# Expert turns on split weights: gate and up in slabs of 512 columns, two weight tiles to a slab

## What is computed

```
def swiglu(h, w_gate, w_up, w_down):
    return (jax.nn.silu(h @ w_gate) * (h @ w_up)) @ w_down

logits = (t @ router).astype(F32)
top_v, top_i = lax.top_k(logits, TOP_K)        # TOP_K = 2 of N_EXPERTS = 8
gates = jax.nn.softmax(top_v, axis=-1)
def run_block(args):
    tok, e = args
    return swiglu(t[tok], w_gate[e], w_up[e], w_down[e])
...
y = jnp.zeros_like(t).at[slot_tok].add(out)
```

## Time and profile before

| | us |
|---|---|
| median of 3 runs | 2563.54 |
| lowest, highest | 2558.66, 2566.74 |
| the profiled execution, its own time | 2564.95 |
| span of the profiled execution | 2563.1 |
| PE busy | 2330.8 (91%) |
| DVE busy | 1191.1 (46%) |
| ACT busy | 926.1 (36%) |

### The profile page before, as it was taken

How to read it: one execution, slowest core, us unless ns; L and a number is a source line. 1 busy time by engine, 2 the same in 40 slices (tenths; PEclk the granted TensorE clock), 3 DMA queues, 4 the chain that set the end, 5 groups by cost and what they waited for, 6 DMA issues and landing times.

```text
span 2563.1 us, 41521 instructions
## 1 busy us (share of the span) xinstructions
PE 2330.8 (91%) x17097; PEld 2067.9 (81%) x17097; DVE 1191.1 (46%) x1606; ACT 926.1 (36%) x1176; POOL 118.5 (5%) x182
## 2 busy tenths in 40 slices
PE   7988999999999777778969999999999999999995
PEld 6864888888778666645959898988899999999995
DVE  3267433232353666534368887888888100001001
ACT  4346322221322333134236666676667000000001
POOL 6010000000000000000000000000000100000000
PEclk9999899999999888889879999999999999999998
DMA  6310232242221000020179999999999877877663
GB/s 183 121 66 17 67 99 88 93 136 91 74 90 38 2 2 2 2 66 1 75 239 339 336 339 336 343 343 343 346 342 320 284 256 240 266 258 249 230 224 115
DMA packets 334011, 452.37 MB, mean 176 GB/s; under 512 B 8392, under 2 KB 291887, under 8 KB 333711
## 3 DMA queue, kind: packets, MB, share of 16 engines
q1 hardware_dynamic: 328896, 435.73, 50.8%
q0 software_dynamic: 4752, 14.00, 2.3%
q10 hardware_dynamic: 190, 0.05, 0.0%
HBM read 437.22 MB, written 12.52 MB: 175 GB/s over the span
## 4 chain that ended last, share of the span: by engine, by line
PE 84%; DVE 7%; ACT 4%; issue 2%; DMA 1%; ACTq 0%; DVEq 0%; POOLq 0%; SPq 0%; POOL 0%
PE bank L668 81%; PE bank L671 4%; DVE arena L1899 2%; DVE slot L1899 1%; DVE w_low L1899 1%; ACT w_high L1816 1%; DVE h_mix L1899 0%; DVE small L1952 0%; ACT arena L1585 0%; ACT w_high L1427 0%; DMA arena<-h_rows_d,idx_ahead 0%; DMA xs<-sum_rows_d 0%; DMA sum_rows_d<-arena,idx_now 0%; ACT arena L1459 0%; DVE arena L2576 0%
## 5 line engine op out<-in xcount | busy, mean ns | idle before, releaser
L1899 DVE TENSOR_TENSOR w_low<-slot,w_high 128x2048 fp32r<-128x2048 f32 x172 | 393.6, 2292 | 314.7 <-ACT w_high L1427 266.4
L668 PE MATMUL bank<-arena 128*128 128x144 f32 (+7 forms) x2608 | 349.6, 300 | 6.4 <-ACT arena L1502 2.6
L668 PE MATMUL bank<-w_high,xg_high 128*128 128x256 f32 x1120 | 325.9, 291 | 11.3 <-issue 4.8
L668 PE MATMUL bank<-arena,slot 128*128 128x144 f32 (+4 forms) x2368 | 313.2, 312 | 20.6 <-ACT slot L1733 14.8
L668 PEld LDWEIGHTS bank<-arena 128*128 128x128 f32 (+4 forms) x2608 | 308.5, 185 | 22.4 <-issue 11.0
L668 PEld LDWEIGHTS bank<-arena,slot 128*128 128x128 f32 (+2 forms) x2368 | 290.4, 189 | 39.8 <-issue 19.7
L668 PE MATMUL bank<-w_low,xg_high 128*128 128x256 f32 x1120 | 318.6, 284 | 0.0
L668 PE MATMUL bank<-w_high,xg_low 128*128 128x256 f32 x1120 | 317.9, 284 | 0.0
L1899 DVE TENSOR_TENSOR arena<-arena,bank 128x256 f32<-128x256 f32 (+3 forms) x134 | 63.8, 476 | 528.7 <-PE bank L668 528.7
L1899 DVE TENSOR_TENSOR w_low<-arena,w_high 128x2048 fp32r<-128x2048 f32 x105 | 240.5, 2291 | 55.7 <-ACT w_high L1816 55.7
L1816 ACT ACTIVATE w_high<-slot 128x2048 fp32r<-128x2048 f32 x108 | 207.0, 1918 | 78.3 <-PE bank L668 49.5
(11 more groups left out here) (365 smaller groups left out, 3398.7 us busy)
## 6 DMA issues: line engine op xcount, KB each, us to landing
slot<-in_moe_w_gate_dram SPq DMA_DIRECT2D x64, 1024.0 KB, 6.1
arena<-in_moe_w_down_dram SPq DMA_DIRECT2D x64, 1024.0 KB, 5.8
slot<-in_moe_w_up_dram SPq DMA_DIRECT2D x56, 1024.0 KB, 5.8
arena<-in_moe_w_up_dram SPq DMA_DIRECT2D x56, 1024.0 KB, 6.5
arena<-in_moe_w_gate_dram SPq DMA_DIRECT2D x48, 1024.0 KB, 5.8
slot<-in_moe_w_down_dram SPq DMA_DIRECT2D x48, 1024.0 KB, 6.3
slot<-in_e_w_in_dram SPq DMA_DIRECT2D x12, 1024.0 KB, 5.6
slot<-in_ff_w_gate_dram SPq DMA_DIRECT2D x11, 1024.0 KB, 5.4
```

Of the source, the lines that this page charges most:

```text
L668: return pe.matmul(o, lhsT, rhs, start=start, stop=True, skip_group_check=True)
L1899: return dve.tensor_tensor(o, a, b, op)
```

## The change

In split turns alone, gate and up are worked in slabs of 512 columns. A slab is two tiles, each of four row blocks (512 rows) by 512 columns, still 1 MB; PE works a tile as 4 x 3 matmuls 512 columns wide, and both tiles add into one full bank. The order (`wide_order`) becomes g0 g1 u0 u1, then six times two g, two u and two d, where the d are those of the slab before; the last two are d12 d13. SiLU and `hid_tok` are formed once a slab, 512 columns wide, into single buffers. `turn_hidden(p-2)` stands behind g(p), and the last two stand behind d10 and d11. At the turn's end ACT takes `hid_high` ahead of `xg_parts`, not behind. The positions (7, 10, 16, 19, 22) of the row work are kept as numbers. The 16 matmuls on the identity ahead of the first turn become 28. The float32 turns are as they were but for their first six loads, which wait for a count that holds after either order (`former_tile_used`).

```
+def wide_order():
+    slab = lambda j: [("g", 2 * j), ("g", 2 * j + 1), ("u", 2 * j), ("u", 2 * j + 1)]
+    w = slab(0)
+    for j in range(1, GROUPS_E // 2):
+        w += slab(j) + [("d", 2 * j - 2), ("d", 2 * j - 1)]
+    return w + [("d", GROUPS_E - 2), ("d", GROUPS_E - 1)]
+def former_tile_used(n):
+    return ([("up_full", FF_TILES)] * 2 + [("down_used", 9)] * 3 + [("down_used", 10)])[n]
...
-                            name, count = expert_tile_used(n - RAW)
+                            name, count = former_tile_used(n) if n < RAW else expert_tile_used(n - RAW)
...
+                        if kind in ("g", "u") and split:
+                            rows, cols = 512 * (j % 2), 512 * (j // 2)
...
-                            for k in range(KT):
-                                m = split_product(b[:, 0:256], (xg_high[:, k, :], xg_low[:, k, :]), (wh[:, k, :], wl[:, k, :]), k == 0)
+                            for k in range(4):
+                                row = 4 * (p % 2) + k
+                                m = split_product(b[:, :], (xg_high[:, row, :], xg_low[:, row, :]), (wh[:, k, :], wl[:, k, :]), row == 0)
...
-                                if j >= 1:
-                                    turn_hidden(j - 1)
+                                if p >= 2:
+                                    turn_hidden(p - 2)
...
-                                if j == GROUPS_E - 1:
-                                    turn_hidden(j)
-                                down(n, j)
+                                down(n, p)
+                                if p in (GROUPS_E - 4, GROUPS_E - 3):
+                                    turn_hidden(p + 2)
...
-                for i in range(16):
+                for i in range(28):
                     mm(acc[0][:, 0:P], ident[:, :], ident[:, :], True)
...
-                            if kind == "g":
-                                act.wait_ge(sem("gate_full"), turn * GROUPS_E + (FF_TILES + j + 1))
-                                act.wait_ge(sem("hid_ready"), turn * GROUPS_E + (FF_TILES + j - 1))
-                                act.activation(sil_e[:, j % 2, 0:256], turn_banks[2 * j % 4][:, 0:256], ACT.Silu)\
+                            if kind == "g" and p % 2 == 1:
+                                act.wait_ge(sem("gate_full"), turn * GROUPS_E + (FF_TILES + p + 1))
+                                act.wait_ge(sem("hid_ready"), turn * GROUPS_E + (FF_TILES + p - 1))
+                                act.activation(sil_wide[:, :], turn_banks[(p - 1) % 4][:, :], ACT.Silu).then_inc(sem("sil_ready"), 2)
...
-                                tt(hid_tok[:, j % 2, :], sil_e[:, j % 2, 0:256], turn_banks[(1 + 2 * j) % 4][:, 0:256], ALU.mult)\
+                                tt(hid_tok[:, :], sil_wide[:, :], turn_banks[p % 4][:, :], ALU.mult).then_inc(sem("hid_ready"), 2)
```

More of the change, by code:

```diff
@@ L481, in expert @@
                     ring = expert_ring(raw_slots, landed, turn)
-                    for n, (kind, j) in enumerate(expert_order()):
+                    for n, (kind, j) in enumerate(wide_order() if split else expert_order()):
                         if split:
@@ L1812, in high @@
                         if ring.turn is not None:
-                            name, count = expert_tile_used(n - SPLIT)
+                            name, count = wide_tile_used(n - SPLIT)
                             act.wait_ge(sem(name), turn * GROUPS_E + count)
@@ L1826, in expert_split @@
                         ring.n = SPLIT
-                        for n, (kind, j) in enumerate(expert_order()):
-                            if kind == "g":
-                                act.wait_ge(sem("gate_full"), turn * GROUPS_E + (FF_TILES + j + 1))
-                                act.wait_ge(sem("hid_ready"), turn * GROUPS_E + (FF_TILES + j - 1))
-                                act.activation(sil_e[:, j % 2, 0:256], turn_banks[2 * j % 4][:, 0:256], ACT.Silu)\
[L1832 to L1837, removed]
+                        for n, (kind, p) in enumerate(wide_order()):
+                            if kind == "g" and p % 2 == 1:
+                                act.wait_ge(sem("gate_full"), turn * GROUPS_E + (FF_TILES + p + 1))
+                                act.wait_ge(sem("hid_ready"), turn * GROUPS_E + (FF_TILES + p - 1))
+                                act.activation(sil_wide[:, :], turn_banks[(p - 1) % 4][:, :], ACT.Silu).then_inc(sem("sil_ready"), 2)
+                            turned = p - 2 if kind == "g" and p >= 2 else p + 2 if kind == "d" and GROUPS_E - 4 <= p < GROUPS_E - 2 else -1
                             if turned >= 0:
@@ L1843, in expert_split @@
                                                ACT.Copy).then_inc(sem("hid_high_ready"), 1)
+                            if n == TILES_E - 3:
+                                act.wait_ge(sem("up_full"), turn * GROUPS_E + (FF_TILES + GROUPS_E))
+                                xg_parts(turn, 1)
                             if n < TILES_E - 2:
@@ L2490, in expert_split @@
                         rows_after = {17: 0, 20: 1, 23: 2}
-                        for n, (kind, j) in enumerate(expert_order()):
-                            turned = j - 1 if kind == "g" else j if j == GROUPS_E - 1 and kind == "d" else -1
+                        for n, (kind, p) in enumerate(wide_order()):
+                            turned = p - 2 if kind == "g" and p >= 2 else p + 2 if kind == "d" and GROUPS_E - 4 <= p < GROUPS_E - 2 else -1
                             if turned >= 0:
```

48 lines of the change are left out of this document (29 added, 19 removed).

## The result

| | before | after |
|---|---|---|
| median of four runs | 2562.47 us | 2541.18 us |
| lowest to highest | 2558.66 to 2566.74 | 2538.34 to 2542.18 |
| the profiled execution's own time | 2564.95 us | 2540.66 us |
| ratio after / before, 95% interval | | 0.9914 (0.9902 to 0.9926) |

The direction was right.

A forecast was written before the change was run, and what follows sets the result against it. PE was taken to set the pace. A turn's terms, -1.5 - 1.1 + 0.7 + 0, gave -1.9 us, five turns -9.5, with the start -10.0: 2555.0 us from the profiled 2564.95, median forecast 2553.5, range 2544 to 2565.

The forecast's parts named there:

- wider matmuls: Gate and up in split turns: 336 matmuls of 512 columns for 672 of 256 save 1.5 us a turn.
- end of the turn: Last turn_hidden behind d11 removes PE's wait for hid_low ahead of d13: 1.1 us less a turn.
- position 7 and g4: DVE's row work delays tile 10's low half, PE waits about 1.5 ahead of g4: net 0.7 us more a turn.
- head: Start of a split turn: SiLU's table load holds up tile 4, 0.75 us replacing a wait of 0.8: nothing net.
- the loop's turn: PE's gap of 2.34 us ahead of g0 with nothing to wait for, carried over unchanged.
- half clock behind it: g0 behind the loop's turn at half clock, 4.45 in place of 2.87: 1.6 us, in no term of the sum.
- rival 1: Clock falls behind the new wait ahead of g4, so a turn gains about 0: 2563 us; chance 0.17.
- rival 3: SiLU and hid_high ahead of the copy for each slab's first down tile make PE wait: 2571 us; chance 0.12.
- Rival 2: Transfers bind at the turn's mean of 339 GB/s, a turn stays at 134 us: 2563 us; chance 0.08.
- -0.5 at the start: Twelve more identity matmuls ahead of the first turn may keep the clock up: 0.5 us less, bounds 0 and 3.3.
- the float32 turns: First loads issued up to three tiles later cost nothing, at most 1 us in each of the three turns.

The follow-up runs named there:

- e9: Changed kernel with the last turn_hidden moved back to straight ahead of d13: 2543.2 us, ratio 0.9923 to the kernel before.
- e1: Kernel before, its order kept, with gate and up matmuls 512 columns wide (body 1234 instructions, products not the reference's): 2539.8 us, ratio 0.9909.
- e2: Changed kernel with eight already satisfied waits ahead of each product of PE's split loop (body 1873 instructions): 2564.2 us, ratio 1.0001.
- e5: Changed kernel with DVE's row work of position 7 split and put later, place_slots at 8 and rows_now at 9: 2533.6 us, ratio 0.9880.
- e6: Changed kernel with one single-column SiLU added at the head of ACT's split turn, ahead of tile 3's copy: 2535.4 us, ratio 0.9885.
- e7: Changed kernel with the edits of e5 and e6 together: 2526.8 us, ratio 0.9854 to the kernel before.
- e10: Changed kernel with the 28 identity matmuls ahead of the first turn put back to 16: 2546.0 us in one run.
- e4: Kernel before with the changed kernel's later counts for each float32 turn's first six loads: stretch across the float32 turn-over 180.97 us, 178.77 before.
- e3: Changed kernel with six already satisfied waits ahead of each product of PE's split loop (body 1705 instructions): 2564.2 us in one run.

## Why the prediction was wrong, step by step

A turn, forecast and measured (133.30 to 127.73, a difference of 5.57):

| step | forecast, us | measured, us | from |
|---|---|---|---|
| wider matmuls | -1.5 | -2.3 | a steady slab 17.46 to 17.13, seven times |
| end of the turn | -1.1 | -1.0 | e9, 128.73 against 127.73 |
| position 7 and g4 | +0.7 | +0.65 | 1.32 now, 0.67 in the earlier trace rows |
| head | 0 | 0 | 0.69 now, 0.66 in the earlier trace rows |
| the loop's turn | not touched | -2.1 | gap of 2.32 in the mean of four to 0.19 |
| half clock behind it | not touched | -0.8 | 1.6 at two of four turn-overs of before |
| sum | -1.9 | -5.55 | |

To the first row belong transposes two slabs apart in after (PE's timeline), to the row on the half clock the 2.3 us behind the third turn-over of before, whose gap of 2.44 was followed by full clock (to be read against the last of the earlier trace rows).

```profile
1395.22 0.38 PE L698 MATMUL bank<-ident,arena 128*128 128x128 f32 x2
...
1429.50 0.38 PE L698 MATMUL bank<-ident,arena 128*128 128x128 f32 x2
```
```profile
1721.50:1723.80 2.30, 2.30 (x19) 2.30 (x20) 2.00 (x1) 0.27 (x1) 1.81 (x2) 1.00 1.08 389
```

**The step that failed** is in the list of PE's waits: the loop's turn, "2.34 with nothing to wait for", and the half clock behind it, 1.6 us. I found the gap, priced it, and then carried it over as a constant ("8.8, d13, the loop's gap"), so that no term of the sum has it. The runs showed PE's branch in its place, 4.8 us with the long body and 0.21 with the short one, and 2.9 of the 5.57 us of a turn are that. I never asked what PE did in the gap. The row of the branch and the instruction queue's eight packets a turn would have answered, and the change takes away 705 of 1906 instructions. e1 and e2 show the cause from both sides: the old order with a short body has no gap, the new order with a long body has it again.

**The second miss** is the matmuls' term. I had 1.7 us from single tiles and 1.3 from the round, and took 1.5. A gain of 0.33 us shows in every slab of six tiles, seven to a turn. The single tiles had it nearly right: 0.24 of the 0.33 is in the four gate and up tiles, and most of the rest in the two down tiles, which now stand together (5.54 us for twice 2.80).

**What held.** The wait at the end of the turn, the new wait ahead of g4, and the head came out within 0.1 us each. e5 and e6 confirm their causes: moving the row work takes away the one, loading the table earlier the other. The clock stayed at 1.00 behind a gap of 1.35, so rival 1 didn't come. Steady slabs run without a wait, so rival 3 (the chain for the first down tile) didn't either. Rival 2 didn't come (e7), and one of its supports was misread: 360 GB/s was not the best of before over 20 us, since 368 were moved from 1506 to 1526 us. In sum the steps I did price were worth -2.65 a turn where I said -1.9.

**Outside the split turns.** -0.5 at the start was nothing (e10), and the float32 turns gave back 2.2 us (e4).

The profiled executions add up: -5.57 x 4 for the turn-overs, -2.6 for the last turn (from position 10 to the first float32 matmul, 99.18 to 96.54 us), +2.2 in the float32 turns, and -1.3 us by which position 10 of the first turn came earlier, nearly all of it in work that the change doesn't touch: -24.0, where the two own times differ by 24.3. The work ahead of the first turn varies by some 7 us from run to run (g0 starts between 1313.5 and 1320.7 us in these profiles), which is why the turn's length is the better measure here.

## What to carry to other kernels

A gap at a loop's end with "issue" as its releaser, or with one that was done long before, is to be looked up in the sequencer's rows: the branch of that engine, and the instruction queue. Where the branch takes microseconds, count the instructions of that engine's body first: in this kernel everything up to 1649 went round in 0.21 us, and 1705 and more cost 4.8 to 7, but for one turn-over. Wider matmuls are then worth more than what they save each, and an edit that adds waits or unrolls a loop can lose the same amount in one step.

## What the runs showed of the hardware

- PE's branch back to the loop's start: 0.21 us for bodies of 1201 to 1649 instructions, 4.7 to 7.1 us for 1705 to 1906 (but for e3's first, 0.26), where a longer body wasn't dearer. The long bodies move 7 to 9 packets a turn on the instruction queue once they are being loaded again, the short ones at most one packet in four turns. ACT's and DVE's take 0.04 to 0.08 us in this kernel.
- The clock behind such a gap isn't set by the gap's length alone: in before, gaps of 2.28 and 2.34 us were followed by a mean of 0.71 and 0.50 over 2.3 us, gaps of 2.44 and 2.22 by 1.00.
- The SiLU's table load displaces that of the copies: with a SiLU first in the turn, one load of 1.28 us serves both.
- 362 GB/s over 126 us, with a DMA share of 1.00 (e7): no engine waited for a landing.
